# Retention of a hybrid encoder layer laid out by head pairs instead of by direction

## The reference, cut to what matters

```
scores = (q k^T) * dmat                        # 128x128 per head, decays of both directions
intra  = scores v
s_f, s_b = (k * w_kf)^T v, (k * w_kb)^T v      # 64x64 per head, forward and backward
st_f, st_b = scans of s_f and s_b over the chunks of a sequence
inter  = (q * w_qf) st_f + (q * w_qb) st_b
ret    = (intra + inter), normalised per head, * gain * silu(gate)
```

## Time and profile before

| what | value |
|---|---|
| median of 3 runs | 1493.01 us (1488.55 to 1494.6) |
| span of the profiled execution | 1489.8 us |
| time of that execution beside its span | not listed; the page gives the span alone |
| PE busy | 1394.8 us, 94% of the span |
| DVE busy | 1085.6 us, 73% |
| ACT busy | 858.9 us, 58% |
| POOL busy | 391.6 us, 26% |
| DMA | 329.28 MB, 221 GB/s |

### The profile page before, as it was taken

The page is one execution under the profiler, slowest core; times in us unless marked ns, Lnnn a source line. Parts: engine busy times, 40 slices in busy tenths (PEclk is TensorE's granted clock), DMA queues, the critical chain, the costliest instruction groups (busy, mean ns, idle before and its releaser), DMA issues.

```text
span 1489.8 us, 22984 instructions
## 1 busy us (share of the span) xinstructions
PE 1394.8 (94%) x8472; PEld 1154.6 (78%) x8472; DVE 1085.6 (73%) x1523; ACT 858.9 (58%) x1030; POOL 391.6 (26%) x282
## 2 busy tenths in 40 slices
PE   6999899999998999998999689999999999999983
PEld 5788788888877788787888568888888777777771
DVE  4766776444568677773666789999988888888876
ACT  6534444334456555553444457777777777777764
POOL 2000111111133000001212235655533333344321
PEclk9999999999999999999999889999999999999996
DMA  8344421222121210014666559999999999999977
GB/s 281 135 144 143 155 82 62 96 85 79 71 93 44 64 51 29 29 57 132 226 230 249 200 208 352 388 388 394 392 391 376 378 378 373 376 387 379 378 278 289
DMA packets 63308, 329.28 MB, mean 221 GB/s; under 512 B 11862, under 2 KB 18406, under 8 KB 50946
## 3 DMA queue, kind: packets, MB, share of 16 engines
q1 hardware_dynamic: 45906, 278.60, 49.1%
q0 software_dynamic: 17328, 49.69, 10.9%
HBM read 285.06 MB, written 51.93 MB: 226 GB/s over the span
## 4 chain that ended last, share of the span: by engine, by line
PE 27%; DMA 15%; issue 4%; DVE 4%; ACT 2%; SPq 0%; POOLq 0%; DVEq 0%; POOL 0%; ACTq 0%
PE acc L96 8%; PE acc L98 8%; PE acc L97 8%; DMA odd_gate<-in_w_gate 7%; DMA odd_rest<-in_w_down 4%; DMA plain<-in_w_gate 4%; ACT shared L1880 2%; DVE split L1897 1%; PE acc L2568 1%; PE acc L2538 1%; PE acc L2097 1%; PE acc L2108 1%; DVE plain L2703 0%; DVE plain L2741 0%; DMA plain<-in_g_ffn 0%
## 5 line engine op out<-in xcount | busy, mean ns | idle before, releaser
L96 PE MATMUL acc<-shared,split 128*128 128x512 f32 x936 | 375.6, 401 | 7.1 <-DVE split L1897 3.3
L98 PE MATMUL acc<-shared,split 128*128 128x512 f32 x936 | 367.5, 393 | 0.0
L96 PEld LDWEIGHTS acc<-shared,split 128*128 128x128 f32 x936 | 177.7, 190 | 43.7 <-DVE split L1897 3.7
L98 PEld LDWEIGHTS acc<-shared,split 128*128 128x128 f32 x936 | 176.9, 189 | 38.0
L96 PE MATMUL pa<-shared,a_xT_hi 128*128 128x512 f32 (+1 forms) x480 | 192.7, 402 | 8.5 <-DVE a_w_lo L741 8.5
L98 PE MATMUL pa<-shared,a_xT_lo 128*128 128x512 f32 (+1 forms) x480 | 186.7, 389 | 0.0
L97 PE MATMUL acc<-even_lo,split 128*128 128x512 f32 x384 | 150.6, 392 | 0.0
L1897 DVE TENSOR_TENSOR even_lo<-plain,shared 128x4096 fp32r<-128x4096 f32 x33 | 145.9, 4421 | 1.2 <-ACT shared L1892 0.6
L1897 DVE TENSOR_TENSOR split<-odd_rest,shared 128x4096 fp32r<-128x4096 f32 x31 | 137.1, 4422 | 6.4 <-ACT shared L1892 5.8
L1892 ACT CAST shared<-plain 128x4096 fp32r<-128x4096 f32 x33 | 119.9, 3635 | 27.3 <-DMA plain<-in_w_up 14.0
L2433 POOL DMA_INDIRECT plain<-s_h_rows,plain x32 | 126.3, 3947 | 18.5 <-PE acc L2538 7.0
(11 more groups left out here) (360 smaller groups left out, 2891.4 us busy)
## 6 DMA issues: line engine op xcount, KB each, us to landing
plain<-in_w_gate SPq DMA_DIRECT2D x24, 2048.0 KB
plain<-in_w_up SPq DMA_DIRECT2D x16, 2048.0 KB
plain<-in_w_down SPq DMA_DIRECT2D x16, 2048.0 KB
odd_rest<-in_w_down SPq DMA_DIRECT2D x16, 2048.0 KB
odd_rest<-in_w_up SPq DMA_DIRECT2D x16, 2048.0 KB, 21.4
odd_gate<-in_w_gate SPq DMA_DIRECT2D x8, 2048.0 KB, 24.6
a_x_turned<-in_x_turned SPq DMA_DIRECT2D x24, 512.0 KB, 3.6
a_x_row<-in_x SPq DMA_DIRECT2D x12, 512.0 KB, 4.7
```

What stands on the lines that cost most here:

```text
L96: pe.matmul(out, st_hi, mv_hi, start=first, stop=False)
L98: return pe.matmul(out, st_lo, mv_hi, start=False, stop=last)
```

## The change

The states lie by head: even heads on partitions 0-63, odd heads on 64-127, with the direction in the free dimension. Queries are held once (`q_tok`, 128 x 512) and turned two heads at a time: 4 transposes, one ACT copy to `qd` (128 x 512), and one DVE multiplication that reads `qd` twice and writes `qs` (128 x 1024). `outputs` keeps its two score matmuls per head (128 rows x 64 columns) and does four on the states in place of two, each 64 rows x 64 columns, into an output that spans two PSUM banks (4 and 5). Copies and scan steps are 128 x 256 instead of 64 x 512. The decay rates of `rate2` come from `rate` on ACT in place of two DMAs; `spans` is 128 x 256. Since banks 4 and 5 are in use longer, the products `m` of `phase_latent` go to banks 0 and 1, and `queries(g)` and the second of `values` wait for both halves of `m`.

```diff
@@ scores and turns
-    pe.wait_ge(s_qd, 2 * t + 2)
+    pe.wait_ge(s_qd, t + 1)
...
-    ins = pe.matmul(pP[odd][:, cols], kv[rows, t % 2, cols], qd[rows, 2 * pair + odd, :],
+    ins = pe.matmul(pP[odd][:, cols], kv[rows, t % 2, cols], qd[rows, pair, :],
                     start=True, stop=True)
...
-    for j in range(4):
-        h = 4 * r + j
-        ins = pe.transpose(pT[:, j * P:(j + 1) * P], tok[:, h].rearrange("p a d -> p (a d)"), ident[:])
+    for j in range(4):
+        ins = pe.transpose(pT[:, j * P:(j + 1) * P], q_tok[:, j * P:(j + 1) * P], ident[:])
@@ own_state
-    for h in range(HR):
+    for j in range(HR // 2):
         for a in range(2):
-            ins = pe.matmul(pS[a * DR:(a + 1) * DR, h * DR:(h + 1) * DR], kw[:, h, a, :],
-                            kv[:, t % 2, 512 + h * DR:512 + (h + 1) * DR], start=True, stop=True)
+            cols = slice((a * HR // 2 + j) * DR, (a * HR // 2 + j + 1) * DR)
+            for odd in range(2):
+                h = 2 * j + odd
+                ins = pe.matmul(pS[odd * DR:(odd + 1) * DR, cols], kw[:, h, a, :],
+                                kv[:, t % 2, 512 + h * DR:512 + (h + 1) * DR], start=True, stop=True)
@@ outputs
-    for h in range(HR):
-        out = [pO[a * DR:(a + 1) * DR, h * DR:(h + 1) * DR] for a in range(2)]
-        half = [slice(a * DR, (a + 1) * DR) for a in range(2)]
-        for a in range(2):
-            pe.matmul(out[a], sc[:, h % 2, h // 2, half[a]], kv[:, t % 2, 512 + h * DR:512 + (h + 1) * DR],
-                      start=True, stop=False)
-        for a in range(2):
-            ins = pe.matmul(out[a], qs[:, h, half[a]], st[t][:, h, :], start=False, stop=True)
+    half = [slice(b * DR, (b + 1) * DR) for b in range(2)]
+    for j in range(HR // 2):
+        for odd in range(2):
+            h = 2 * j + odd
+            for b in range(2):
+                pe.matmul(pO[half[b], odd, j, :], sc[:, odd, j, half[b]],
+                          kv[:, t % 2, 512 + h * DR:512 + (h + 1) * DR], start=True, stop=False)
+        for a in range(2):
+            for odd in range(2):
+                for b in range(2):
+                    ins = pe.matmul(pO[half[b], odd, j, :], qs[half[odd], a, j, half[b]],
+                                    st[t][half[odd], a, j, :], start=False, stop=a == 1)
@@ the query loop on PE
-    turn_queries(t, 0)
+    turn_queries(t)
     if t:
         outputs(t - 1)
-    if t + 1 == N:
-        turn_queries(t, 1)
...
     project(G, n, pG, low)
-    if t + 1 < N:
-        turn_queries(t, 1)
-    else:
+    if t + 1 == N:
         scores(t)
     project(G, n, pG, high).then_inc(s_pg, 1)
@@ ACT
-    ins = nc.scalar.copy(st[t + 1][0:DR].rearrange("p h d -> p (h d)"), pS[0:DR, :])
+    ins = nc.scalar.copy(st[t + 1][:, 0].rearrange("p j d -> p (j d)"), pS[:, 0:256])
...
-    nc.scalar.copy(qd[:, 4 * r:4 * r + 4, :].rearrange("p h i -> p (h i)"), pT[:]).then_inc(s_qd, 1)
+    nc.scalar.copy(qd[:].rearrange("p j i -> p (j i)"), pT[:]).then_inc(s_qd, 1)
@@ DVE
-    a4, b4 = (y.unsqueeze(2).broadcast_to([P, HR, 2, DR]) for y in (a3, b3))
-    return nc.vector.tensor_tensor(tok[:], a4, b4, ALU.add)
+    return nc.vector.tensor_tensor(k_tok if n < N else q_tok, part1[:], part2[:], ALU.add)
...
-    nc.vector.tensor_tensor(qs[:, 4 * r:4 * r + 4, :], qd[:, 4 * r:4 * r + 4, :],
-                            wqT[:, 4 * r:4 * r + 4, :], ALU.mult).then_inc(s_qs, 1)
+    nc.vector.tensor_tensor(qs, qd.unsqueeze(1).broadcast_to([P, 2, HR // 2, P]), wqT, ALU.mult).then_inc(s_qs, 1)
...
-    nc.vector.memset(st[first][0:DR], 0.0)
-    nc.vector.memset(st[first + tiles - 1][DR:P], 0.0).then_inc(s_zero, 1)
+    nc.vector.memset(st[first][:, 0], 0.0)
+    nc.vector.memset(st[first + tiles - 1][:, 1], 0.0).then_inc(s_zero, 1)
@@ phase_latent
+    m_bank = [ps[0][:, 0:512], side[0]]
...
+    elif i == 1:
+        pe.wait_ge(s_mlo, 2)
...
-    pe.wait_ge(s_mlo, h // 2 + 1)
+    pe.wait_ge(s_mlo, 2)
```

More of the change, by code:

```diff
@@ L248, in phase_project @@
                 if t > first and not last_of(t):
-                    scan_steps.append((t, slice(0, DR), t, t + 1))
+                    scan_steps.append((t, 0, t, t + 1))
                 if last_of(t):
-                    scan_steps += [(t, slice(DR, P), i + 1, i) for i in range(t - 2, first - 1, -1)]
+                    scan_steps += [(t, 1, i + 1, i) for i in range(t - 2, first - 1, -1)]
         TAIL = sum(1 for step in scan_steps if step[0] == N - 1)
@@ L391, in take_last @@
             act.wait_ge(s_rst, 16 * (N - 1))
-            nc.scalar.copy(retT, pO[:]).then_inc(s_rtev, 1)
+            nc.scalar.copy(retT, pR[:]).then_inc(s_rtev, 1)
         def bank_of_turned(pe):
@@ L599, in take_own @@
                 if not last_of(t):
-                    ins = nc.scalar.copy(st[t + 1][0:DR].rearrange("p h d -> p (h d)"), pS[0:DR, :])
+                    ins = nc.scalar.copy(st[t + 1][:, 0].rearrange("p j d -> p (j d)"), pS[:, 0:256])
                 if not first_of(t):
-                    ins = nc.scalar.copy(st[t - 1][DR:P].rearrange("p h d -> p (h d)"), pS[DR:P, :])
+                    ins = nc.scalar.copy(st[t - 1][:, 1].rearrange("p j d -> p (j d)"), pS[:, 256:512])
                 ins.then_inc(s_ownev, 1)
             def tables():
-                act.wait_ge(s_tabs, 160)
-                nc.scalar.activation(rate[:], rate[:], ACT.Exp)
-                nc.scalar.activation(rate2[:], rate2[:], ACT.Exp).then_inc(s_rate, 1)
-                act.wait_ge(s_rate, 1)
+                act.wait_ge(s_tabs, 128)
+                for odd in range(2):
+                    rows = slice(odd * DR, (odd + 1) * DR)
+                    nc.scalar.activation(rate2[rows].rearrange("p (a j) -> p a j", a=2),
+                                         rate[rows].rearrange("p a (j o) -> p o a j", o=2)[:, odd], ACT.Exp).then_inc(s_rate, 1)
+                act.wait_ge(s_rate, 2)
+                nc.scalar.activation(rate[:], rate[:], ACT.Exp).then_inc(s_rate, 1)
+                act.wait_ge(s_rate, 3)
                 for d in range(2):
@@ L614, in decays @@
             def decays():
-                for h in range(HR):
-                    ins = nc.scalar.activation(wqT[:, h, :], spans, ACT.Exp, scale=rate2[:, h:h + 1])
+                for a in range(2):
+                    for j in range(HR // 2):
+                        one = slice(a * HR // 2 + j, a * HR // 2 + j + 1)
+                        ins = nc.scalar.activation(wqT[:, a, j, :], spans[:, a], ACT.Exp, scale=rate2[:, one])
                 ins.then_inc(s_exps, 1)
@@ L710, in _ @@
                 latent_norm(t)
-                take_queries(t, 0)
+                take_queries(t)
                 if t:
@@ L803, in scan @@
                 for i in due:
-                    _, rows, a, b = scan_steps[i]
+                    _, way, a, b = scan_steps[i]
                     dve.wait_ge(s_ownev, t + 1)
@@ L855, in decayed, with weigh_queries @@
                                         dmat[:, odd].rearrange("p a i -> p (a i)"), ALU.mult).then_inc(s_sc, 1)
-            def weigh_queries(t, r):
-                dve.wait_ge(s_qd, 2 * t + r + 1)
+            def weigh_queries(t):
+                dve.wait_ge(s_qd, t + 1)
                 if t:
@@ L951, in _ @@
                 latent(t)
-                weigh_queries(t, 0)
+                weigh_queries(t)
                 if t:
@@ L958, in _ @@
                     normalise(t - 1)
-                weigh_queries(t, 1)
                 if t < TAIL // 2:
```

89 lines of the change are left out of this document (42 added, 47 removed).

## The result

The changed kernel takes 1496.06 us (median of 7 runs, 1492.07 to 1501.54), the kernel before 1492.83 us beside it (7 runs): ratio 1.0044, 95% interval 1.0028 to 1.0059. The ratio is not that of the two medians, which would be 1.0022. A second comparison gave 1493.35 us (12 runs) and 1.0012, 0.9996 to 1.0028. The profiled execution took 1495.56 us, its span is 1494.1. So the changed kernel is slower by 0.1 to 0.4%. The second interval just reaches no change, and only the upper end of the first lies beyond 0.5%.

What follows compares the result with a forecast made beforehand. PE's instruction list was taken to bound the query loop. Key loop -0.7 and -0.8, first tile +0.3, ten tiles -4.4, last tile -1.4, form changes +10.8 make +3.8 us on 1493.0: 1496.8 us, range 1484 to 1508.

Steps and rivals of the forecast that it cites:

- What bounds the loop: Query loop: PE's list of instructions sets the time in ten tiles; gains on DVE and ACT there are worth nothing.
- The seams: In `outputs`: seven changes between matmuls of 128 and 64 rows per tile, 0.14 us each, 10.8 us over eleven tiles.
- Rival 1: In `outputs`: matmuls of 128 and 64 rows follow each other without a stop, 10.8 us absent, 1486.0 us; chance 20%.
- The quarters: In `outputs`: four quarters of PE's array run at once, 0.015 us per 64*64 record, costing what the replaced records cost.
- Rival 2: In `outputs`: array quarters run two at a time, 0.94 us more per tile, 1507.7 us; 20% including dearer form changes.
- The transposes: Query loop: one group of four fewer per tile, 0.44 us each, 4.4 us saved over the ten middle tiles.
- The twelfth `outputs`: Behind the query loop: PE's 1.30 us wait for POOL hides the 0.98 us that form changes add here.
- The first tile: First query tile: DVE's longer `weigh_queries`, then `lo_of_x`, delay the next projection; nothing gained, 0.3 us lost.
- The key loop: Loop over keys: shorter memsets at its start save 0.7 us, a shorter wait at its end 0.8 us.
- Rival 3: After the key loop's two shorter waits PE keeps its clock, about 3 us back each time, 1491 us; chance 5%.
- The sum: Whole kernel: -7.0 us of savings and +10.8 us for form changes make +3.8 us, 1496.8 us; chance 55%.
- Behind the barrier.: After the latent attention's barrier: no difference should arise; earlier changes carry one to one to the end.

## Why the prediction was right, point by point

- **What bounds the loop.** Right: in the middle tiles PE has no gap before or after, and a tile grew by what PE's list grew, 0.627 us (0.98 - 0.44 = 0.54 forecast). Some 11 us less work on DVE and 6 us less on ACT over ten tiles bought nothing there.
- **The seams.** Right in kind, and 0.145 to 0.162 us each instead of 0.14, by three orders of the same matmuls (seven, four, one). With the group of transposes at 0.473, seven cost 0.627 + 0.473 = 1.10 us per tile, 0.98 forecast. Rival 1, no seams, is out. What happens in the array at a change no run shows, only its price.
- **The quarters.** Right: 0.0146 us a record, four at once. Rival 2 is out, by 0.94 us per tile.
- **The transposes.** 0.47 us a group for 0.44, so 4.7 us for 4.4 over ten tiles. From the `turn_latent` of the last tile but one to that of the last it takes 23.01 us for 23.44: 0.43 us less, where the prediction's 1.4 off and 0.98 on gave 0.42.
- **The twelfth `outputs`.** Right: PE's wait for POOL went from 1.30 to 0.22 us, and the last two turns are 13.37 us apart in both kernels.
- **The first tile.** The order of cause was right (DVE's `weigh_queries`, then `lo_of_x`). The wait for `lo_of_x` is absent in the changed kernel's first profile, 0.52 us in its second and up to 1.1 us in its variants. The group's wait of 1.01 us, from which the prediction started, is itself not constant: 0.22 us in the third profile of the kernel before. The two tiles from the last keys on took 37.5 and 37.6 us for 36.6 to 37.3 before. The prediction's 0.3 for this tile and 0.54 for the next make 0.84; some 0.5 came.
- **The key loop.** Here a term was mis-sized. The start: memsets of 256 elements follow each other in 0.27 us; from the first memset to the turn of the first keys it takes 3.45 us for 4.74, 1.3 us less where 0.8 was taken, and 0.2 us per memset was too little. But of these 1.3, part is cut off by ACT's exponentials (0.8 in the changed kernel's second profile, where the first states gained 0.45 us only). "The extra exponential on ACT is ready before DVE asks for it" was wrong. In one profile DVE waited 0.75 us for ACT. In the other ACT ended at 35.08 and DVE began at 35.11, 0.74 us after the start of the instruction before, where 0.61 us is the distance in the kernel before (37.39 to 38.00): it was held there too, by some 0.13 us. The end: the wait is 0.96 us shorter, where the sum took 0.8 and the sign named for it 1.1. The whole loop took 167.1 and 168.9 us for a mean of 171.3: 3.3 us less where 1.5 was forecast. One part of the rest is the clock. Over 30 to 50 us the granted clock is 0.83 in all four profiles of the kernel before and in seven of the ten with the new layout, and 0.91 in the other three, the changed kernel's first among them. That is 3.4 and 1.8 us of the full clock lost in 20 us. The key loop takes 166.5 to 167.4 us in these three, 168.3 to 169.9 in the seven. Rival 3 gets no more than this: the length of the wait ahead does not sort them (2.63 us before one of the three, 2.71 before one of the seven), and behind the second wait the clock is 0.83 over 170 to 190 us in all fourteen. The other part is the start of DVE's chain, which varies too.
- **The sum.** From the turn of the last keys to the last turn 270.7 us for a mean of 265.0: +5.7 us, where the steps gave 0.3 - 4.4 - 1.4 + 10.8 = +5.3. With the key loop's 3.3 us off, that is +2.4 in all, for the +3.8 of the prediction. Part of this closeness is luck: nine middle tiles grew by 0.8 us more than forecast, and the key loop shrank by 1.8 us more, in part by the clock. The two comparisons gave +6.6 us (0.44% of 1492.83; the medians alone +3.2) and +1.8 (0.12% of 1491.6), and the forecast lies between them. The range's lower end, rival 1 with the key loop at its best, adds up to 1485.0 and not to 1484.
- **"Behind the barrier."** The prediction called itself wrong in kind if the difference arose there. In the first pair of profiles it did, by 5.6 us. The second pair turned it round, and the code there is the same: one pair of profiles can't carry such a reading.

## What to carry to other kernels

When rows of a state are split so that the products take half the rows, sort the matmuls by their form: the price is not in the number of records but in each change between forms, and with a start flag on the first matmul of a bank alone the scores can all go before the states. Here that turned +0.1 to +0.4% into -0.2%, and with `lo_of_x` ahead of a product that nobody awaits into -0.3 to -0.5%. Where PE's list gets shorter, look at who runs beside whom behind it: 2.7 us of the loop's gain were taken back where one DVE instruction was held by POOL. Before you believe a difference of the whole, look at a stretch that PE alone sets, and see whether it repeats.

## What the runs showed of the hardware that I had not expected

- A run of POOL instructions held one DVE instruction with two inputs from SBUF for 5.18 us in four profiles of three kernels, until 0.55 us after the run of nine was over. With POOL's start moved behind it, it took 0.68 us. The Trainium skill ("SBUF — State Buffer", "Who interferes with whom") says that such a DVE instruction contends with a POOL instruction that reads SBUF, and that the order of issue decides who blocks. The traces agree that either can be the one that is held: in the other nine profiles DVE took 0.68 or 0.69 us, and POOL's first instruction 1.23 or 1.24 instead of 0.72. They do not show the order of issue, since DVE's record starts first in all thirteen, by 0.03 to 0.06 us. And DVE was held by all nine instructions, not by one.
- A change between two forms costs about 0.15 us in either direction, also where only the rows change (128*64 to 64*64). The Trainium skill's rule on this ("TensorEngine Tiling (Array Packing)", "Tiling Modes"), that a change of the tiling mode drains the array, fits this price; it has no figure.
- The stretches at the low clock differ between executions of the same code: the granted clock over 30 to 50 us was 0.91 in one profile of the changed kernel and 0.83 in the other, and the key loop took 167.1 and 168.9 us.
